# Two layers of a streaming encoder on one core: six of eight gate blocks as seven-product jobs

## The reference, cut to what matters

```python
x = half_swiglu(x, ffn1)                     # RMSNorm, up 1024->2*2816, silu, down, x += 0.5 * ...
h = rms_norm(x, mix_norm)
q, k, v, qi, ki, wi, cb, cc, cx, gates = split_cols(h @ w_in)
o_att = sparse_attention(...)                # (T, 512), rope, indexer, top-k keys, softmax
o_conv = cb * conv3(cc * cx)                 # (T, 512)
y_a = o_att  @ w_branch[:512]
y_b = o_conv @ w_branch[512:]
g_a, g_b = split(sigmoid(gates))             # each (T, 1024)
x = x + (g_a * y_a + g_b * y_b) @ w_out
x = half_swiglu(x, ffn2)
```

## Time and profile before

| | us |
|---|---|
| median of 3 runs | 2683.68 |
| the profiled execution | 2684.65 |
| its span in the trace | 2682.8 |
| PE busy | 2649.2 (99%) |
| DVE busy | 2053.6 (77%) |
| ACT busy | 1347.9 (50%) |
| POOL busy | 924.3 (34%) |
| granted PE clock, mean | 0.997 |

### The profile page before, as it was taken

The page is one execution under the profiler, slowest core; times in us unless marked ns, Lnnn a source line. Parts: engine busy times, 40 slices in busy tenths (PEclk is TensorE's granted clock), DMA queues, the critical chain, the costliest instruction groups (busy, mean ns, idle before and its releaser), DMA issues. The chain is left out here.

```text
span 2682.8 us, 48331 instructions
## 1 busy us (share of the span) xinstructions
PE 2649.2 (99%) x18372; PEld 2584.4 (96%) x18372; DVE 2053.6 (77%) x3489; ACT 1347.9 (50%) x2498; POOL 924.3 (34%) x642
## 2 busy tenths in 40 slices
PE   9999999999999999999999999999999999999997
PEld 8999999998999999999999999999989999999997
DVE  8998976886433799988789989678773337989985
ACT  5555555536322355555555555464463224555553
POOL 1243333355433303343302433333544332043432
PEclk9999999999999999999999999999999999999999
DMA  3222223233122222222222222222332221222222
GB/s 129 87 90 85 80 75 101 89 122 125 62 78 86 71 76 91 79 95 80 79 79 79 85 89 79 77 91 92 133 110 72 70 94 63 77 97 79 91 83 71
DMA packets 89786, 234.31 MB, mean 87 GB/s; under 512 B 8816, under 2 KB 42352, under 8 KB 89072
## 3 DMA queue, kind: packets, MB, share of 16 engines
q1 hardware_dynamic: 74784, 204.11, 21.9%
q10 hardware_dynamic: 14800, 27.51, 2.9%
HBM read 223.32 MB, written 8.27 MB: 86 GB/s over the span
## 5 line engine op out<-in xcount | busy, mean ns | idle before, releaser
L589 POOL TENSOR_TENSOR w_lo<-w_raw,w_hi 128x1024 fp32r<-128x1024 f32 (+1 forms) x178 | 372.4, 2092 | 622.9 <-ACT w_hi L1264 607.1
L643 POOL TENSOR_TENSOR lo_A<-raw_even,hi_A 128x512 fp32r<-128x512 f32 (+1 forms) x168 | 231.3, 1377 | 641.6 <-ACT hi_A L1320 640.6
L723 PE MATMUL lin<-h_hi,w_hi 128*128 128x320 f32 x1600 | 374.9, 315 | 8.2 <-DVE tmp L1822 2.8
L1264 ACT ACTIVATE w_hi<-w_raw 128x1024 fp32r<-128x1024 f32 (+1 forms) x174 | 168.5, 969 | 419.2 <-PE lin L723 290.2
L723 PE MATMUL lin<-h_hi,w_lo 128*128 128x320 f32 x1600 | 364.9, 309 | 0.0
L723 PE MATMUL lin<-h_lo,w_hi 128*128 128x320 f32 x1600 | 364.8, 309 | 0.0
L643 POOL TENSOR_TENSOR lo_A<-raw_odd,hi_A 128x512 fp32r<-128x512 f32 (+1 forms) x156 | 234.1, 1501 | 372.5 <-ACT hi_A L1320 372.3
L723 PEld LDWEIGHTS lin<-h_hi,w_hi 128*128 128x128 f32 x1600 | 265.3, 189 | 22.1 <-issue 14.6
L723 PEld LDWEIGHTS lin<-h_lo,w_hi 128*128 128x128 f32 x1600 | 268.2, 188 | 0.0
L723 PEld LDWEIGHTS lin<-h_hi,w_lo 128*128 128x128 f32 x1600 | 267.9, 188 | 0.0
L888 PE MATMUL bank<-h_hi,hi_A 128*128 128x320 f32 x704 | 217.6, 309 | 0.0
(11 more groups left out here) (420 smaller groups left out, 7806.7 us busy)
## 6 DMA issues: line engine op xcount, KB each, us to landing
w_raw<-wts SPq DMA_DIRECT2D x144, 512.0 KB, 3.3
raw_even<-wts SPq DMA_DIRECT2D x80, 512.0 KB, 4.0
raw_odd<-wts SPq DMA_DIRECT2D x72, 512.0 KB, 4.0
raw_even<-wts SPq DMA_DIRECT2D x48, 384.0 KB, 3.6
raw_odd<-wts SPq DMA_DIRECT2D x48, 384.0 KB, 3.6
w_raw<-wts SPq DMA_DIRECT2D x32, 256.0 KB, 2.6
caches<-kcache_in ACTq DMA_DIRECT2D x16, 512.0 KB, 3.7
caches<-vcache_in ACTq DMA_DIRECT2D x16, 512.0 KB, 4.5
```

What stands on the lines that cost most here:

```text
L589: ins = nc.gpsimd.tensor_tensor(w_lo[:, s, cols], w_raw[:, s, cols], w_hi[:, s, cols].bitcast(F), ALU.subtract)
L643: nc.gpsimd.tensor_tensor(strip_lo[name][:, cols], raw_pair[k % 2][:, block_, cols], strip_hi[name][:, cols].bitcast(F), ALU.subtract).the ...
L723: ins = nc.tensor.matmul(out[:, half, :], w, a[:, half * HALF:(half + 1) * HALF], start=first and n == 0, stop=last and n == 2)
L1264: nc.scalar.activation(w_hi[:, s, 0:cols], w_raw[:, s, 0:cols], ACT.Copy).then_inc(hi_ready.sem, 1)
```

## The change

`GATE_PLAIN = 2` gate blocks stay plain. The other `GATE_JOBS = 6` (per layer) become jobs: the two gate tiles of an output block as seven products, and the branch tile in two parts inside the job, after M7 and after M3. For this:

- The mixing norm's tokens are scaled in place in `x` (8 instructions on DVE), so `x` is first stored in HBM (`x_kept`, one DMA of all 8 blocks early in the projections) and read back in two DMAs, once four and once all eight of the `m` blocks have been split.
- DVE makes T1 to T4 and all the strips' lo parts and sums of the gate jobs, and the lo part of the branch weights. POOL only makes the lo parts of the plain tiles (`GATE_AT + 2` to `+ 5`) and then of the out tiles.
- `m` is kept in `x` and split only late: blocks 0 to 3 and 4 to 6 in the last job, block 7 after it.
- The hardware loops over the gate blocks go; their instructions are written out.
- `closing`: the strips of the next part's first job come one row earlier, and in every closing DVE now does `norm_block(6)` before it adds row 7. Several start-up semaphores are merged.

```diff
+                for i in range(GATE_JOBS):                                  # PE
+                    if i == 0:
+                        pe.wait_ge(evacuated.sem, evacuated.count(L, OUT_RES))
+                        pe.wait_ge(B_ready.sem, B_ready.count(L, 3 + 1))
+                    else:
+                        pe.wait_ge(gated.sem, gated.count(L, 2 * GATE_PLAIN + 4 * i - 3))
...
+                    gate_product(L, i, "M1", job_banks(i)[0], "A11", [z[:, 0:4, 0:HALF] for z in (h_hi, h_lo)], True)
...
+                    gate_product(L, i, "M5", job_banks(i)[2], "S1", [z["T1"] for z in (T_hi, T_lo)], True)
...
+                    pe.wait_ge(m1_in_middle.sem, m1_in_middle.count(L, NJ + i + 1))
+                    gate_product(L, i, "M6", job_banks(i)[1], "S2", [z["T2"] for z in (T_hi, T_lo)], False)
...
+                    gate_product(L, i, "M2", job_banks(i)[0], "A12", [z[:, 4:8, 0:HALF] for z in (h_hi, h_lo)], False)
...
+                    pe.wait_ge(u_one_kept.sem, u_one_kept.count(L, NJ + i + 1))
+                    gate_product(L, i, "M7", job_banks(i)[1], "S3", [z["T3"] for z in (T_hi, T_lo)], False)
+                    branch(L, i, 0)
...
+                    gate_product(L, i, "M4", job_banks(i)[1], "A22", [z["T4"] for z in (T_hi, T_lo)], False)
...
+                    gate_product(L, i, "M3", job_banks(i)[2], "S4", [z[:, 4:8, HALF:T] for z in (h_hi, h_lo)], False)
+                    branch(L, i, 1)
...
+                for j in range(GATE_PLAIN):                                 # ACT
+                    for g in range(2):
+                        if g:
+                            if j == 0:
+                                split(L, GATE_AT + 3)
+                            else:
+                                gate_strip(L, 0, "S1")
+                                gate_strip(L, 0, "A22")
+                        act.wait_ge(evacuated.sem, evacuated.count(L, GATE_RES + 2 * j + g + 1))
+                        nc.scalar.activation(tmp[:, g, :], tmp[:, g, :], ACT.Sigmoid).then_inc(gated.sem, 1)
+                    if j == 0:
+                        split(L, GATE_AT + 4)
+                        gate_T(L, "T1")
+                        split(L, GATE_AT + 5)
+                        gate_T(L, "T2")
+                        gate_T(L, "T3")
+                        gate_T(L, "T4")
+                gate_strip(L, 0, "A11")
+                gate_B(L, 0)
+                gate_strip(L, 0, "S2")
+                gate_B(L, 1)
+                gate_B(L, 2)
+                gate_strip(L, 0, "S4")
+                gate_strip(L, 0, "A12")
+                gate_strip(L, 0, "S3")
+                branch_hi(L, 0)
+                for i in range(GATE_JOBS):
+                    act.wait_ge(product_done["M1"].sem, product_done["M1"].count(L, q + 1))
...
+                    nc.scalar.activation(job_banks(i)[1], job_banks(i)[0], ACT.Copy).then_inc(m1_in_middle.sem, 1)
...
+                        gate_strip(L, i + 1, "A11")
+                        gate_strip(L, i + 1, "S1")
...
+                    nc.scalar.activation(gate(2, early), job_banks(i)[1], ACT.Copy).then_inc(u_one_kept.sem, 1)
...
+                dve.wait_ge(x_spilled.sem, x_spilled.count(L, 16))           # DVE, after g_lo of L2651
+                for c in range(4):
+                    scale_row(c)
+                leave(L, GATE_AT, 0, 0, tmp[:, 0, :], r[:, :])
+                for c in range(4, KB):
+                    scale_row(c)
+                gate_add_tokens(L, "T1")
+                gate_add_tokens(L, "T3")
+                leave(L, GATE_AT + 1, 0, 1, tmp[:, 1, :], r[:, :])
+                gate_add_tokens(L, "T2")
+                gate_lo_T(L, "T1")
+                gate_add_tokens(L, "T4")
+                gate_add(L, 0, "S1")
+                gate_add(L, 0, "S2")
+                gate_add(L, 0, "S3")
+                make_plain(0)
+                gate_lo_T(L, "T2")
+                leave(L, GATE_AT + 3, 0, 0, tmp[:, 0, :], r[:, :])
+                gate_lo_T(L, "T3")
+                gate_lo_T(L, "T4")
+                gate_lo(L, 0, "S1")
+                gate_lo(L, 0, "A22")
+                leave(L, GATE_AT + 4, 0, 1, tmp[:, 1, :], r[:, :])
+                gate_lo(L, 0, "A11")
+                gate_lo_B(L, 0)
+                gate_lo(L, 0, "S2")
+                gate_add(L, 0, "S4")
+                gate_lo_B(L, 1)
+                make_plain(1)
+                gate_lo(L, 0, "A12")
+                gate_lo(L, 0, "S3")
+                branch_lo(L, 0)
+                gate_lo(L, 0, "S4")
+                gate_lo_B(L, 2)
...
+                for i in range(GATE_JOBS):
+                        gate_lo(L, i + 1, "A11")
+                        gate_add(L, i + 1, "S1")
...
+                pair_free(L, FFN2_Q - 1)                                     # SP, after the last job's loads
+                for n in range(2):
+                    sp.dma_start(w_raw[:, n, :], wts[...]).then_inc(raw_in[n], 16)
+                pair_free(L, FFN2_Q - 2)
+                load_job(L, FFN2_Q, FFN_WEIGHTS + MIX_WEIGHTS)
+                sp.wait_ge(m_ready.sem, m_ready.count(L, 4))
+                sp.dma_start(x[:, 0:4, :], x_kept[:, 0:4, :]).then_inc(x_landed[0], 16)
+                sp.wait_ge(m_ready.sem, m_ready.count(L, KB))
+                sp.dma_start(x[:, 4:KB, :], x_kept[:, 4:KB, :]).then_inc(x_landed[1], 16)
+                for n in range(2, KB):
+                    load(L, OUT_AT + n, FFN_WEIGHTS + PROJ + 3 * KB + n)
```

`make_plain(j)` is two multiplications from `bank` and one addition. The functions which the jobs call:

```diff
+            def gate_product(L, i, name, out, strip_, tokens, opens):
+                pe.wait_ge(strip_ready[strip_].sem, strip_ready[strip_].count(L, NJ + i + 1))
+                w = (strip_hi[strip_], strip_lo[strip_])
+                for c in range(4):
+                    for n, (a, b) in enumerate(((0, 0), (0, 1), (1, 0))):
+                        ins = nc.tensor.matmul(out, w[a][:, c * P:(c + 1) * P], tokens[b][:, c, :], ...)
+                ins.then_inc(product_done[name].sem, 1)
```

More of the change, by code:

```diff
@@ L330, in S2_sum, with job_banks, y_banks, gate_S2 @@
             return lin[1][:, i % 2, :] if i else S2_first[:, :]
+        def job_banks(i):
+            return [bank[:, k, 0:HALF] if i else lin[k // 2][:, k % 2, 0:HALF] for k in range(3)]
+        def y_banks(i):
+            return [lin[k][:, :, 0:HALF] if i else bank[:, 2 * k:2 * k + 2, 0:HALF] for k in range(2)]
+        def gate_S2(i):
+            return (S2_first[:, :], lin[1][:, 1, :])[i] if i < 2 else bank[:, 3, :]
+        def m_row(j):
+            if j < 4:
+                rows, cols = 2 * (j % 2), (slice(HALF, T) if j < 2 else slice(0, HALF))
+                return x[:, rows:rows + 2, cols]
+            return halves(x[:, j, :])
         def quarters(ap):
@@ L1805, in _, with gate @@
-                closing(L, OUT_AT, OUT_RES, 2, (L, NJ))
+                def gate(row, cols):
+                    return tmp[:, row, cols]
+                early, late = slice(0, HALF), slice(HALF, T)
+                for j in range(GATE_PLAIN):
+                    for g in range(2):
+                        if g:
+                            if j == 0:
+                                split(L, GATE_AT + 3)
+                            else:
+                                gate_strip(L, 0, "S1")
[9 more added lines that the diff above has]
+                        gate_T(L, "T4")
@@ L1806, in _ @@
+                keep_m(L, KB - 1)
+                split(L, OUT_AT + 2)
+                closing(L, OUT_AT, OUT_RES, 2, (L, FFN2_Q))
                 act.wait_ge(tails_stored.sem, tails_stored.count(L, 16))
@@ L1887, in closing @@
                 for j in range(KB):
-                    last = (L, p, j) == (DEPTH - 1, 3, KB - 2)
+                    last = j == KB - 2
                     if j + 1 < KB and not last:
@@ L2669, in _, with scale_row, weigh_y @@
-                closing(L, OUT_AT, OUT_RES, 2, 1.0, (L, NJ))
+                dve.wait_ge(x_spilled.sem, x_spilled.count(L, 16))
+                def scale_row(c):
+                    nc.vector.scalar_tensor_tensor(out=x[:, c, :], in0=x[:, c, :], scalar=gain[:, c:c + 1], in1=r[:, :],
+                                                   op0=ALU.mult, op1=ALU.mult).then_inc(h_scaled_done.sem, 1)
+                def weigh_y(j, part_):
+                    n = GATE_AT + 3 * j + 3
+                    dve.wait_ge(gated.sem, gated.count(L, 2 * j + 2))
+                    dve.wait_ge(tile_done.sem, tile_done.count(L, n))
+                    nc.vector.tensor_tensor(halves(tmp[:, part_, :]), bank[:, 2 * part_:2 * part_ + 2, 0:HALF],
+                                            halves(tmp[:, part_, :]), ALU.mult).then_inc(mixed.sem, 1)
@@ L2670, in _ @@
+                lo_m(L, KB - 1)
+                closing(L, OUT_AT, OUT_RES, 2, 1.0, (L, FFN2_Q))
                 ffn(L, 1, FFN2_AT, FFN2_RES)
```

466 lines of the change are left out of this document (350 added, 116 removed).

## The result

The changed kernel takes 2698.47 us (median of 4 runs, 2696.56 to 2703.15) against 2683.68: the ratio is 1.0058, 95% interval 1.0045 to 1.0070. It is slower by 14.8 us; the forecast's sum was +12.9, to 2697. The profiled execution took 2698.08 us, its span is 2696.1. One execution of the kernel before, beside a later experiment, took 4308.13 us at a granted clock of 0.555 and stands in no comparison here.

A forecast was written before the change was run, and what follows sets the result against it. PE's matmuls were taken to bound the kernel, with DVE's queue late at the stage's entry. -21.1 + 2 x (14.2 + 1.0 + 2.0) - 0.4 = +12.9 us gave 2697 us, range 2680 to 2708.

The forecast's parts named there:

- -21.1 for the matmuls, settled jobs at nothing: Gate stages: 144 fewer matmuls on PE save 21.1 us; settled jobs cost nothing, ACT's M6 copy having 0.9 us margin.
- Rival 2: Settled gate jobs fall behind since ACT's M6 copy stands behind the next job's strip: 2709 to 2712 us, chance 0.13.
- The entry, 14.2: Gate stage start: DVE's queue makes M7 of job 0 late; 11.2 us plus 3.0 of hand-overs per layer.
- my 3.0 of hand-overs: Gate stage entry: waiting for ACT, whose order is chained to DVE's, adds 3.0 us per layer.
- The lock: Gate stage entry: POOL's three weight tiles and DVE hold SBUF in turn, so DVE stands still 7.2 us.
- rival 4: Gate stage entry milder, POOL overlapping with half of it: 5 us less per layer, 2687 us, chance 0.17.
- Rival 1: Gate stage entry: DVE keeps up and the change pays, -9 to -13 us, 2671 to 2675; chance 0.11 with everything faster than -5.4.
- Clock +1.0 per layer: After PE's long waits the clock falls to half; only that after M7 counts, 1.0 us with what lies outside these windows.
- The exit, 2.0: Last gate job: POOL's out tile delays DVE's lo parts of m and the multiplication freeing `lin[0]`; PE 2.0 us late.
- Closings, start-up and loops -0.4: Outside the gate stages: out closing's sum of squares no longer waits, 0.2 us per layer; bounds -0.4 to +1 in all.
- The residual in HBM at nothing: Storing x and reading it back costs nothing; at most 2 us at the projections and 3 at out tile 2.
- rival 3: SP's queue: reading x back delays out tile 2, the store the projections; up to 5 us per layer, 2700 to 2707, chance 0.12.

The follow-up runs named there:

- The run with the sets: The changed kernel with POOL setting weight tiles `GATE_AT + 3` to `+ 5` to zero instead of subtracting: 2687.82 us, 3.5 over the kernel before.
- the two fastest versions: The changed kernel with all edits together and ACT's splits ahead, with the old closings (2669.26 us) and with the new closings (2671.39 us).
- the version without long waits in the stage: The changed kernel with all edits together, old closings included, and ACT's splits ahead: 2669.26 us, ratio 0.9947 to the kernel before.

## Why the prediction was right, step by step

- **-21.1 for the matmuls, settled jobs at nothing**: right. PE's instructions are 18228, and PE waits for nothing in jobs 1 to 5. Rival 2 is out.
- **The entry, 14.2**: measured 13.7. By wait, forecast and measured: `GATE_AT + 3` 1.5, 1.43; `+ 4` 1.6, 1.26; branch 1 2.4, 1.95; M1 4.0, 3.54; M6 0.9, none seen or 0.55; M7 3.8, 3.59 in the layer whose clock held until then. The mechanism is the one forecast. The chain was DVE's queue, and the runs which shortened it moved M7 by as much.
- **The entry's parts** are less good than their sum. From 705.88 to the sum of S1 for job 1 DVE took 47.9 us. Of these 39.1 are work (38.3 forecast), 5.5 standing still (7.2 forecast: each DVE instruction lost 1.1 to 2.2 us and not all of POOL's 2.4 to 2.8) and 3.3 idle time for ACT. I had no idle time on DVE and named its absence as a sign; my 3.0 of hand-overs stood between ACT, POOL and PE. That the sum still fits within 0.5 us is partly luck. The lock's smaller size is a piece of rival 4, 1.7 of its 5 us per layer.
- **Rival 1** put -9 to -13 us on the case that POOL's tiles meet nobody and ACT's chain runs beside. The run with the sets made the first half of that case, and was still 3.5 us slower than before: the lock is the largest single part of the loss and not enough alone.
- **Clock +1.0 per layer**: mis-sized, and near by luck. I took 21 matmuls for 4 us against 27, 0.9 us for a fall. But a window also counts the matmuls that only reach into it: at full clock it lists 15 or 16 for 2 us, as in the last window above, with the old closing, where 13.6 fit. By the granted clock of the earlier trace rows a fall costs 1.7. It costs nothing where it lies inside the chain. In this profile one fall of the first layer lies there, and two of the second layer count, behind M7 and behind the wait before out tile 0: 3.4 against 2.0. A further one, in the second FFN's closing, stands in the profiles of both kernels.
- **The exit, 2.0**: 1.86 and 1.85, ended by the multiplication at 865.02, which DVE made behind three lo parts (3.85 us in place of 2.3, beside POOL's instruction from 860.54 to 862.94).
- **Closings, start-up and loops -0.4**: the sum was right by luck. In the profile all that lies outside the gate stages is -0.3 without the clock, but it is made of +1.73 in the second FFN's closing and of -0.80 before the first branch tile, -0.42, -0.18 and -0.65 elsewhere, which no run took apart. For the closings alone the step was wrong: the two fastest versions have +1.8 to +2.1, outside the bounds of -0.4 to +1, where a fall of the clock comes with them, and about 0.5 by the waits alone. The step counted the wait that `norm_block(6)` removes at the out closing, and not that in the second FFN's closing the same block stands before row 7, so that the sum of squares comes later there.
- **The residual in HBM at nothing**, rival 3: no wait was seen at out tile 2 or at the projections' tiles; ACT did wait 7.7 us for the weight tile behind the reading back (split at 875.90) without PE noticing. No run took this part away alone.

In all, -21.1 + 2 x (13.7 + 1.9) + 3.4 - 0.3 = +13.2 against the span's 13.3.

## What to carry over

Before moving work onto an engine at a stage's edge, list its queue there and compare its end with the first instruction that needs it; the waits in between are shares of one lateness and don't add. Mend the chain's last link (the copy before M7) and its queue, not the waits that the profile shows first. Idle time of one engine isn't room if another is working from the same memory then, and a subtraction that the busy engine does itself in 1.2 us can be cheaper than one that stops it for 2.

## What the hardware showed that I hadn't expected

- The lock works both ways: POOL's subtraction took 1.1 to 2.2 us from DVE and was itself stretched from 2.41 to 2.81 and 2.93; with eight scalings in a row beside seven POOL instructions DVE ran at half its pace (13.0 us for 6.5).
- The kernels with long waits in the stage scatter more. The changed kernel and its single edits spread over 3.7 to 8.7 us, the kernel before over 0.8 to 2.8 in its groups of 4 to 21 executions, the version without long waits in the stage over 0.7 (5 executions). That the falls of the clock make the scatter is likely, not shown. In the profiles a fall of the clock behind such a wait costs 1.7 us, or 3.4 behind some. It comes after a wait of 1.95 us in one kernel and not in another: 0.82, 0.50, 0.83 in three windows after 732 us with the old closings put back alone, none there in the changed kernel, with the same wait of 1.95. What decides it stays open.
